# Expert weight pairs in six pairs of places instead of four, and the adding step cut into two halves around the next up products

## The chip, the cores and the metric

The kernel runs on one core of one Trainium2 chip. The time is the device time of one execution in microseconds (us); the runs of the kernel before took 2776.48 us in the median of three (2775.92 to 2777.67). Profiles come from one profiled execution.

## The reference

Two transformer blocks run one after the other over 256 tokens of width 1024, all in float32. The first has feed-forward layers, a gated delta rule and sparse attention. The second, over 272 rows (16 meta tokens ahead), is: fox attention, a mixture of experts, a gated recurrence (hg), a mixture of experts. Only the two mixtures matter here:

```python
def hier_moe(h, w_grp, b_grp, w_rt, b_rt, w_up, w_down):
    ...
    e_val, e_idx = lax.top_k(e_logit, TOP_K)          # 2 of 32 experts per token
    gate = jax.nn.softmax(e_val, axis=-1) * g_gate
    ...
    def expert_block(args):
        xb, e = args
        gate_up = xb @ w_up[e]                        # 1024 x 1024
        a, u = jnp.split(gate_up, 2, axis=-1)
        return (jax.nn.silu(a) * u) @ w_down[e]       # 512 x 1024
    ...
```

Each mixture reads the weights of all 32 experts, 6 MB each in float32.

## The kernel before

**Weights.** All weights come from HBM as slabs of 128 partitions x 2048 float32 (1 MB), in one fixed order, `plan`. SP alone issues their DMAs, in that order (L546 for two slabs at once, L550 for one). They land in `ring`, which has RING = 8 places; slab i goes to place i % 8, and `load(i)` first waits for the semaphore value at which slab i - 8 has been used. SP stands at that wait, and everything behind it in SP's queue stands too.

**The expert slabs** are loaded two by two, 2 MB a DMA. In this text a *pair* is such a DMA, numbered from 0 in each mixture. Pairs 0 and 1 are the up weights of expert 0 (rows 0 to 511, then 512 to 1023 of the 1024), pairs 2 and 3 those of expert 1. Then, for e = 1, 2, ...: two up pairs of expert e + 1 and one down pair of expert e. Pair 94, the last one, is the down pair of expert 31. The down weights of expert 0 are apart (`aside`, L559, two DMAs of 1 MB): before pair 4 SP waits until the sum of squares of the mixture's norm is there (`ss_ready`), and then loads them into the storage of `sq` and a part of `arena`. So the ring holds four pairs, and pair j waits for the products of pair j - 4.

**The order on TensorE** (sparse_pe) is written out by hand. For each expert e: `up_part(e + 1, 0)` (L1331, 16 products with an up pair), `turn(e)` (L1340, two transposes), `combine(e - 1)` (L1372, the adding step: four times, i = 0 to 3, a spread of expert e - 1's result over the tokens, into two banks of PSUM each), `up_part(e + 1, 1)` (L1331), for e < 3 a part of a gather (L1296), and `down_part(e)` (L1356, 16 products with the down pair). The first product of each of these waits for its own slab. Four of PSUM's banks serve the adding step, so its steps i = 2 and 3 wait until VectorE has added i = 0 and 1:

```python
                        if n >= 4:
                            pe.wait_ge(s["moe_x"], MOE_ADDS * l + 2 * (n - 2))
```

**On VectorE** (sparse_dve) each expert has `take_turn(e)` (L3026), `add(e - 1)` (L3047, four additions onto x), `gate_rows(e)` (L3033 twice, L3039) and `hidden_e(e + 1)` (L3019). **On ScalarE** (sparse_act): SiLU (L2100), the rows of expert e + 2 (L2093), and the result of the down products out of PSUM (L2106, `take_y`).

**Ahead of the experts** the mixture is normed, routed (L1402, the transposes of `h` at L1250, marked "htok") and sorted. In the waits of the sort, `keep_clock` (L1256) runs products that nobody reads, with `h` as operand. A second version of each mixture, dense_pe and its like, runs only when an expert has more than 64 rows. It did not run here: the lines of the profile are those of the sparse one.

`sq`, `hid` and `sil` are scratch of the norms, the feed-forward, the attention and hg; the sparse mixture touches none of them after its norm.

Of the kernel before, what the change touches and what calls it, by code (L numbers as in the profile page):

```python
# [8 lines left out]
P = 128  # L9
D = 1024  # L10
KC = D // P
# [171 lines left out]
def arrivals(plan):  # L183

    count, out = [0] * RING, []
    for i in range(len(plan)):
        slot = i % RING - (1 if i and paired(plan, i - 1) else 0)
        if slot == i % RING:
            count[slot] += 1
        out.append((slot, 16 * count[slot]))  # L190
    return out
# [254 lines left out]
def build(nc, ap, stages, marks):  # L446
    plan = slab_plan(stages)
    free, arrive = releases(plan), arrivals(plan)
    with ExitStack() as ctx:
# [12 lines left out]
        sq = sb("sq", [P, KC, T2])  # L462
        hid = sb("hid", [P, 2, 2, T2])
        sil = sb("sil", [P, 2, T2])
# [13 lines left out]
        def view(at, *shape, whole=arena):  # L478
            n = int(np.prod(shape))
            v = whole[:, at:at + n]  # L480
            if len(shape) == 1:
# [7 lines left out]
                 (sq.rearrange("p k n -> p (k n)")[:, 0:SLAB], view(21264, SLAB))]  # L489
# [12 lines left out]
        slot_loaded = [sem(f"slot{i}_loaded") for i in range(RING)]  # L502
# [5 lines left out]

        def slab_view(i, k=KC):
            return ring[:, i % RING, :].rearrange("p (k n) -> p k n", k=k)  # L510

        def low_view(i, k=KC):
            return ring_parts[:, i % RING, :].rearrange("p (k n) -> p k n", k=k)
# [12 lines left out]
        def _(sp):  # L526
# [11 lines left out]
            def load(i):  # L538
                if i >= RING:
                    name, value = free[i - RING]  # L540
                    sp.wait_ge(s[name], value)
                if paired(plan, i):
                    name, value = free[i + 1 - RING]
                    sp.wait_ge(s[name], value)
                    both = ap["slabs"][i:i + 2].rearrange("n p w -> (n p w)").rearrange("(p w) -> p w", p=P)
                    sp.dma_start(ring[:, i % RING:i % RING + 2, :].rearrange("p n w -> p (n w)"), both)\  # L546
                        .then_inc(slot_loaded[i % RING], 16)
                    return
                w = slab_width(plan[i])
                sp.dma_start(ring[:, i % RING, 0:w], ap["slabs"][i, :, 0:w]).then_inc(slot_loaded[i % RING], 16)  # L550

            edges = list(itertools.accumulate(len(slab_plan([st])) for st in stages))
            moe_at = {at - 6 * NE + 2 + RING: q for q, (at, st) in enumerate(zip(edges, stages)) if st[0] == "moe"}
            for i in range(len(plan)):
                if i in moe_at:
                    q = moe_at[i]
                    sp.wait_ge(s["ss_ready"], sum(r[0] != "ada" for r in stages[:q + 1]))
                    for hh in range(2):
                        sp.dma_start(aside[hh].rearrange("p k n -> p (k n)"), ap["aside"][2 * stages[q][1] + hh])\  # L559
                            .then_inc(s["aside_in"], 16)  # L560
                if not (i and paired(plan, i - 1)):
                    load(i)
# [125 lines left out]
        HTLO = 18144  # L688
        LG, SEL, GOH, GCAND, GEXP, EL, ECAND, EL2, TOP1, TOP2 = (RT, RT + 108, RT + 236, RT + 248, RT + 260, RT + 272,
# [47 lines left out]
        def sum_slab(eng, i):  # L737
# [3 lines left out]
            wt = ring[:, i % RING, :].rearrange("p (f k) -> p f k", f=2)  # L741
# [9 lines left out]
        def _(pe):  # L751
# [6 lines left out]
            def slab_in(i):  # L758

                slot, at = arrive[i]  # L760
                pe.wait_ge(slot_loaded[slot], at if trip[0] is None else trip[0] * (24 // RING * 16) + at)
# [3 lines left out]
            def run_jobs(q, st, lo, hi, slab, job, rhs=h, h_at=None, behind=False):  # L765
# [3 lines left out]
                for i, (kind, idx, sl, c0, _) in list(enumerate(stage_jobs(st)))[lo:hi]:  # L769
# [51 lines left out]
                    elif kind in ("vtok", "gba", "fv", "hv"):  # L821
# [3 lines left out]
                        if kind == "gba":  # L825
                            wt = ring[:, nth_slab(st, slab, sl) % RING, 0:KC * 32].rearrange("p (k n) -> p k n", k=KC)
# [485 lines left out]
            def sparse_pe(q, l, slab):  # L1312
# [66 lines left out]
                for e in range(NE):  # L1379
# [3 lines left out]
                    if e:  # L1383
                        combine(e - 1)
# [2022 lines left out]
```

## Time and profile before

| | |
|---|---|
| median of 3 runs | 2776.48 us |
| the profiled execution, its time | 2777.99 us |
| its span | 2776.2 us |
| what lies around the span | 1.8 us |
| mean granted TensorE clock | 0.98 |
| bytes read from HBM | 697.46 MB |
| DMAs of 2 MB, one of 1 MB | 190 and 278 |

The span is cut into 40 slices of 69.4 us in the page's second part. The first mixture lies in slices 23 to 29 (about 1534 to 2038 us), the second from slice 33 to the end (2264 to 2773 us). A busy share there is an average over the slice.

### The profile page before, as it was taken

How to read it: one execution, taken by the hardware profiler on the slowest of the kernel's cores; microseconds unless marked ns; L12 is line 12 of the kernel's file. 1: busy time of each engine (PE TensorE's matmuls, PEld its weight loads, DVE VectorE, ACT ScalarE, POOL GpSimd, SP SyncE). 2: the span in 40 equal slices, each digit the busy share in tenths (PEclk: the TensorE clock that was granted, in tenths of full speed). 3: DMA queues.
4: the chain of work that ended last, by engine and by line, in shares of the span. 5: the costliest groups of instructions: out<-in, count | busy, mean ns of one | idle time of the engine just before them, and what ended most of it. 6: DMA issues, size and time to landing. Idle time of an engine off the chain costs nothing.

```text
span 2776.2 us, 44780 instructions
## 1 busy us (share of the span) xinstructions
PE 2624.0 (95%) x18738; PEld 1897.1 (68%) x18738; DVE 1387.0 (50%) x2815; ACT 767.8 (28%) x1478; POOL 0.2 (0%) x4
## 2 busy tenths in 40 slices
PE   7999989999999989999999999999999999999998
PEld 7999868999999868998777533333367784333333
DVE  7875865776773764753233433333324542323333
ACT  4331444344331353433233211101112331111010
POOL 0000000000000000000000000000000000000000
PEclk9999989999999999999999999999999999999999
DMA  9877301774776311554211599999961238999997
GB/s 365 319 269 275 122 33 64 293 293 189 309 278 245 120 51 62 213 197 159 84 61 47 227 398 428 427 428 427 428 251 60 92 122 325 419 429 427 428 427 316
DMA packets 72353, 701.51 MB, mean 253 GB/s; under 512 B 8784, under 2 KB 11472, under 8 KB 11728
## 3 DMA queue, kind: packets, MB, share of 16 engines
q1 hardware_dynamic: 72144, 698.54, 62.8%
q8 instruction: 154, 2.52, 0.4%
q14 instruction: 55, 0.45, 0.0%
HBM read 697.46 MB, written 1.05 MB: 252 GB/s over the span
## 4 chain that ended last, share of the span: by engine, by line
PE 85%; DVE 6%; DMA 4%; ACT 3%; issue 2%; SPq 0%; DVEq 0%; ACTq 0%
PE ps L1331 15%; PE ps L837 12%; PE ps L1532 9%; PE ps L1530 9%; PE ps L1531 8%; PE ps L1356 7%; PE ps L1372 4%; DMA ring<-slabs 4%; PE ps L828 4%; PE ps L1084 2%; DVE x L3047 2%; PE ps L1509 1%; PE ps L819 1%; PE ps L804 1%; PE ps L1261 1%
## 5 line engine op out<-in xcount | busy, mean ns | idle before, releaser
L1530 PE MATMUL ps<-arena_parts 128*128 128x256 f32 x2032 | 575.8, 283 | 0.4 <-DVE arena_parts L3210 0.4
L1532 PE MATMUL ps<-arena_parts,ring_parts 128*128 128x256 f32 x2032 | 573.2, 282 | 0.0
L1531 PE MATMUL ps<-arena_parts 128*128 128x256 f32 x2032 | 571.5, 281 | 0.0
L1331 PE MATMUL ps<-ring,arena 128*64 128x512 f32 x2048 | 469.0, 599 | 42.7 <-ACT arena L2106 30.3
L1531 PEld LDWEIGHTS ps<-arena_parts 128*128 128x128 f32 x2032 | 385.9, 190 | 0.2
L1530 PEld LDWEIGHTS ps<-arena_parts 128*128 128x128 f32 x2032 | 383.4, 189 | 0.8 <-DVE arena_parts L3210 0.6
L1532 PEld LDWEIGHTS ps<-arena_parts,ring_parts 128*128 128x128 f32 x2032 | 382.7, 188 | 0.0
L1331 PEld LDWEIGHTS ps<-ring,arena 128*64 128x64 f32 x2048 | 147.8, 137 | 326.2 <-issue 260.6
L3199 DVE TENSOR_TENSOR ring_parts<-ring,arena_parts 128x2048 fp32r<-128x2048 f32 x132 | 300.8, 2290 | 109.1 <-ACT arena_parts L1723 108.9
L1723 ACT CAST arena_parts<-ring 128x2048 fp32r<-128x2048 f32 x132 | 250.4, 1905 | 302.1 <-DMA ring<-slabs 295.1
L837 PE MATMUL ps<-h,ring 128*128 128x256 f32 (+1 forms) x1408 | 328.4, 391 | 3.7 <-DVE h L3191 3.5
L837 PEld LDWEIGHTS ps<-h,ring 128*128 128x128 f32 x1408 | 266.4, 192 | 49.9 <-issue 5.3
L3026 DVE COPY arena<-ps 128x256 f32<-128x256 f32 x64 | 27.2, 424 | 459.3 <-PE ps L1340 459.3
L1356 PE MATMUL ps<-ring,arena 128*64 128x512 f32 x992 | 223.7, 593 | 0.0
L2100 ACT ACTIVATE arena<-ps 128x256 f32<-128x256 f32 x64 | 24.6, 384 | 662.9 <-PE ps L1331 662.9
L3047 DVE TENSOR_TENSOR x<-ps,x 128x544 f32<-128x544 f32 x256 | 173.5, 720 | 41.8 <-PE ps L1372 26.8
L1372 PE MATMUL ps<-arena 64*128 64x272 f32 x1024 | 163.0, 428 | 29.3 <-DVE x L3047 27.2
L744 DVE CUSTOM_DVE_ANT_0 ring<-ring,arena,vectors 128x1024 f32<-128x1024 f32 x144 | 176.9, 1279 | 10.1 <-DMA ring<-slabs 10.1
L1356 PEld LDWEIGHTS ps<-ring,arena 128*64 128x64 f32 x992 | 70.7, 137 | 139.5 <-issue 139.0
L1372 PEld LDWEIGHTS ps<-arena 64*128 64x128 f32 x1024 | 82.6, 185 | 94.6 <-DVE x L3047 75.7
L828 PE MATMUL ps<-ring,h 128*128 128x256 f32 (+3 forms) x576 | 115.2, 357 | 0.0
L828 PEld LDWEIGHTS ps<-ring,h 128*128 128x128 f32 (+1 forms) x576 | 84.6, 175 | 22.9 <-issue 2.6
(415 smaller groups left out, 2545.5 us busy)
## 6 DMA issues: line engine op xcount, KB each, us to landing
ring<-slabs SPq DMA_DIRECT2D x190, 2048.0 KB, 14.8
ring<-slabs SPq DMA_DIRECT2D x278, 1024.0 KB, 5.3
sq<-aside SPq DMA_DIRECT2D x2, 1024.0 KB, 8.6
arena<-aside SPq DMA_DIRECT2D x2, 1024.0 KB, 10.7
x<-xT SPq DMA_DIRECT2D x1, 1024.0 KB, 5.6
outT<-x SPq DMA_DIRECT2D x4, 256.0 KB, 2.7
constants<-const SPq DMA_DIRECT2D x1, 875.0 KB, 7.7
vectors<-vec SPq DMA_DIRECT2D x1, 647.5 KB, 7.2
```

Source lines behind the costliest of these rows:

```text
L744: ins = nc.vector.tensor_tensor_reduce(out=wt[:, f], in0=wt[:, f], in1=cond_row, scale=1.0, scalar=col("ada_b", l * NADA + n), op0=ALU.mul ...
L828: mm = nc.tensor.matmul(ps[0:size, b, 0:width], rhs[:, k, at:at + size], wt[:, k, c0:c0 + width], start=(k == 0), stop=(k == KC - 1))
L837: mm = nc.tensor.matmul(bank(b, n), wt[:, k, c0:c0 + P], rhs[:, k, 0:n], start=(k == ks[0]), stop=(k == ks[-1]))
L1331: mm = nc.tensor.matmul(ps[W * hh:W * hh + W, e % 2, :], rows_of, wt[:, c], start=(k == 0 and c == 0), stop=(k == 1 and c == 3))
L1356: mm = nc.tensor.matmul(ps[W * dh:W * dh + W, 3, :], hide[:, e % 2, j, W * hh:W * hh + W], wt[:, j, 512 * dh:512 * dh + 512], start=(hh == ...
L1372: mm = nc.tensor.matmul(ps[:, 4 + 2 * (i % 2) + dh, 0:T2], ysb[rows64, e % 2, i * P:(i + 1) * P], ge[rows64, e % 2], start=True, stop=True)
L1530: nc.tensor.matmul(out, w_hi, v_hi, start=start, stop=False, skip_group_check=True)
L1531: nc.tensor.matmul(out, w_hi, v_lo, start=False, stop=False, skip_group_check=True)
L1532: return nc.tensor.matmul(out, w_lo, v_hi, start=False, stop=stop, skip_group_check=True)
L1723: nc.scalar.copy(hi_slab(i), slab_view(i)).then_inc(s["w_hi"], 1)
L3047: nc.vector.tensor_tensor(two, ps[:, b:b + 2, 0:T2], two, ALU.add).then_inc(s["moe_x"], 4)
L3199: nc.vector.tensor_tensor(low_view(i), wt, hi_slab(i).bitcast(F32), ALU.subtract)\
```

## The change

- `places(plan)` gives each slab its place in place of i % 8. In a mixture the pairs go round over six pairs of places: pairs 0 to 3 of each six take the next eight places of the ring, pairs 4 and 5 take four new places (8, 9 and 10, 11) in a tensor `more`. All other slabs go round the ring as before. `load(i)` waits for the slab that had the place before, `before_it[i]`.
- `sq`, `hid` and `sil` become views of the upper half of `more` (places 10 and 11). The room comes from `dynamic_dma_scratch_size=1024`.
- SP's order: pair 4 is loaded ahead of pair 0. Where pair 4 stood nothing is done. Where pair 5 stood, SP waits for `ss_ready`, loads pair 5, then the first aside slab, waits until the last transposes of `h` are done, and loads the second aside slab, now over `h`.
- From e = 4 on, `combine(e - 1)` does i = 0 and 1 ahead of `up_part(e + 1, 1)` and i = 2 and 3 behind it. VectorE's `add` is cut the same way, around `gate_rows(e)`.
- `keep_clock` reads constants. The dense version gets its own copies of `h`, `hid` and `sil`.

```diff
+def places(plan):
+
+    out, at, n = [], 0, 0
+    for i, s in enumerate(plan):
+        n = (n + 1 if i and plan[i - 1][0] in ("eup", "edown") else 0) if s[0] in ("eup", "edown") else 0
+        if s[0] in ("eup", "edown") and n // 2 % 6 >= 4:
+            out.append(RING + 2 * (n // 2 % 6 - 4) + n % 2)
+        else:
+            out.append(at % RING)
+            at += 1
+    return out
...
+def earlier(place):
+
+    last, out = {}, []
+    for i, p in enumerate(place):
+        out.append(last.get(p))
+        last[p] = i
+    return out
+
+
+def arrivals(plan, place):
+
+    count, out = [0] * (RING + 4), []
+    for i, p in enumerate(place):
+        second = i and paired(plan, i - 1)
+        count[p - 1 if second else p] += 0 if second else 1
+        out.append((p - 1 if second else p, 16 * count[p - 1 if second else p]))
     return out
...
-    free, arrive = releases(plan), arrivals(plan)
+    place = places(plan)
+    free, arrive, before_it = releases(plan), arrivals(plan, place), earlier(place)
...
-        sq = sb("sq", [P, KC, T2])
-        hid = sb("hid", [P, 2, 2, T2])
-        sil = sb("sil", [P, 2, T2])
+        more = sb("more", [P, 4, SLAB])
+        wide = more[:, 2:4, :].rearrange("p n w -> p (n w)")
+        sq = wide[:, 0:KC * T2].rearrange("p (k n) -> p k n", k=KC)
+        hid = wide[:, KC * T2:(KC + 4) * T2].rearrange("p (a b n) -> p a b n", a=2, b=2)
+        sil = wide[:, (KC + 4) * T2:(KC + 6) * T2].rearrange("p (a n) -> p a n", a=2)
...
         aside = [v.rearrange("p (k n) -> p k n", k=2) for v in
-                 (sq.rearrange("p k n -> p (k n)")[:, 0:SLAB], view(21264, SLAB))]
+                 (view(21264, SLAB), h.rearrange("p k n -> p (k n)")[:, 0:SLAB])]
...
-        slot_loaded = [sem(f"slot{i}_loaded") for i in range(RING)]
+        slot_loaded = [sem(f"slot{i}_loaded") for i in range(RING + 4)]
...
+        def slab_place(i, n=1):
+
+            p = place[i]
+            return ring[:, p:p + n, :] if p < RING else more[:, p - RING:p - RING + n, :]
+
         def slab_view(i, k=KC):
-            return ring[:, i % RING, :].rearrange("p (k n) -> p k n", k=k)
+            return slab_place(i)[:, 0].rearrange("p (k n) -> p k n", k=k)
...
             def load(i):
-                if i >= RING:
-                    name, value = free[i - RING]
+                if before_it[i] is not None:
+                    name, value = free[before_it[i]]
                     sp.wait_ge(s[name], value)
                 if paired(plan, i):
-                    name, value = free[i + 1 - RING]
-                    sp.wait_ge(s[name], value)
+                    if before_it[i + 1] is not None:
+                        name, value = free[before_it[i + 1]]
+                        sp.wait_ge(s[name], value)
                     both = ap["slabs"][i:i + 2].rearrange("n p w -> (n p w)").rearrange("(p w) -> p w", p=P)
-                    sp.dma_start(ring[:, i % RING:i % RING + 2, :].rearrange("p n w -> p (n w)"), both)\
-                        .then_inc(slot_loaded[i % RING], 16)
+                    sp.dma_start(slab_place(i, 2).rearrange("p n w -> p (n w)"), both).then_inc(slot_loaded[place[i]], 16)
                     return
                 w = slab_width(plan[i])
-                sp.dma_start(ring[:, i % RING, 0:w], ap["slabs"][i, :, 0:w]).then_inc(slot_loaded[i % RING], 16)
+                sp.dma_start(ring[:, place[i], 0:w], ap["slabs"][i, :, 0:w]).then_inc(slot_loaded[place[i]], 16)
             edges = list(itertools.accumulate(len(slab_plan([st])) for st in stages))
-            moe_at = {at - 6 * NE + 2 + RING: q for q, (at, st) in enumerate(zip(edges, stages)) if st[0] == "moe"}
+            moe_at = {at - 6 * NE + 2: q for q, (at, st) in enumerate(zip(edges, stages)) if st[0] == "moe"}
             for i in range(len(plan)):
                 if i in moe_at:
-                    q = moe_at[i]
+                    load(i + 8)
+                if i - 8 in moe_at:
+                    continue
+                if i - 10 in moe_at:
+                    q = moe_at[i - 10]
                     sp.wait_ge(s["ss_ready"], sum(r[0] != "ada" for r in stages[:q + 1]))
+                    load(i)
                     for hh in range(2):
+                        if hh:
+                            sp.wait_ge(s["pe_step"], marks.value("pe_step", (q, "htok", 5)))
                         sp.dma_start(aside[hh].rearrange("p k n -> p (k n)"), ap["aside"][2 * stages[q][1] + hh])\
                             .then_inc(s["aside_in"], 16)
-                if not (i and paired(plan, i - 1)):
+                elif not (i and paired(plan, i - 1)):
                     load(i)
...
-            wt = ring[:, i % RING, :].rearrange("p (f k) -> p f k", f=2)
+            wt = ring[:, place[i], :].rearrange("p (f k) -> p f k", f=2)
...
-                    nc.tensor.matmul(bank(b, T2), ident, h[:, 0, 0:T2], start=True, stop=True)
+                    nc.tensor.matmul(bank(b, T2), ident, const[:, 0:T2], start=True, stop=True)
...
-                def combine(e):
-                    if e < 3:
-                        await2("act", q, "xs", 1, PIECES[e][-1])
-                    await2("act", "ysb", e)
-                    await2("dve", "ge", e)
-                    for i in range(4):
+                def combine(e, pairs):
+                    if pairs[0] == 0:
+                        if e < 3:
+                            await2("act", q, "xs", 1, PIECES[e][-1])
+                        await2("act", "ysb", e)
+                        await2("dve", "ge", e)
+                    for i in pairs:
                         n = 8 * e + 2 * i
                         if n >= 4:
                             pe.wait_ge(s["moe_x"], MOE_ADDS * l + 2 * (n - 2))
...
@@ -1381,9 +1419,11 @@
                         up_part(e + 1, 0)
                     turn(e)
                     if e:
-                        combine(e - 1)
+                        combine(e - 1, (0, 1) if e > 3 else range(4))
                     if e + 1 < NE:
                         up_part(e + 1, 1)
+                    if e > 3:
+                        combine(e - 1, (2, 3))
                     if e < 3:
                         if e == 0:
                             await2("dve", "rows")
@@ -1392,7 +1432,7 @@
                         gather(q, 1, mark2, lambda engine, *key: (await2 if engine == "act" else await_)(engine, *key),
                                (4, 5, 6, 7), PIECES[e])
                     down_part(e)
-                combine(NE - 1)
+                combine(NE - 1, range(4))
...
-                                    mm = nc.tensor.matmul(bank(b + f, T2), wt[:, c, at:at + P], h[:, 4 * kk + c, 0:T2],
+                                    mm = nc.tensor.matmul(bank(b + f, T2), wt[:, c, at:at + P], dense_h[:, 4 * kk + c],
...
+                await2("dve", "h")
...
-                def add(e):
-                    for i in range(4):
+                def add(e, pairs):
+                    for i in pairs:
                         await2("pe", "add", e, i)
                         if e:
                             dve.wait_ge(s["moe_x"], MOE_ADDS * l + 2 * (8 * (e - 1) + 2 * i + 2))
...
@@ -3053,11 +3094,13 @@
                 for e in range(NE):
                     take_turn(e)
                     if e:
-                        add(e - 1)
+                        add(e - 1, (0, 1) if e > 3 else range(4))
                     gate_rows(e)
+                    if e > 3:
+                        add(e - 1, (2, 3))
                     if e + 1 < NE:
                         hidden_e(e + 1)
-                add(NE - 1)
+                add(NE - 1, range(4))
...
+                for c in range(KC):
+                    ins = nc.vector.scalar_tensor_tensor(out=dense_h[:, c], in0=x[:, c], scalar=col("moe_g", KC * l + c),
+                                                         in1=rstd[:, 0:T2], op0=ALU.mult, op1=ALU.mult)
+                mark2(ins, "h")
...
-        nc = bacc.Bacc("TRN2", target_bir_lowering=False, num_devices=1)
+        nc = bacc.Bacc("TRN2", target_bir_lowering=False, num_devices=1, dynamic_dma_scratch_size=1024)
```

## Rows read from the trace of the kernel before

**Rows 1.** The page's second part: busy tenths, clock, DMA and GB/s in 40 slices.
```profile
PE   7999989999999989999999999999999999999998
...
PEclk9999989999999999999999999999999999999999
DMA  9877301774776311554211599999961238999997
GB/s 365 319 269 275 122 33 64 293 293 189 309 278 245 120 51 62 213 197 159 84 61 47 227 398 428 427 428 427 428 251 60 92 122 325 419 429 427 428 427 316
```

**Rows 2.** Windows of both mixtures: busy us, then PEclk, DMA share, GB/s.
```profile
1533.00:1565.00 32.00, 28.35 (x156) 20.44 (x156) 19.28 (x67) 9.08 (x21) 0.00 (x0) 0.95 0.33 129
1565.00:1613.00 48.00, 47.14 (x249) 21.37 (x246) 13.47 (x25) 5.88 (x14) 0.00 (x0) 1.00 0.90 349
1613.00:1640.00 27.00, 26.15 (x135) 9.96 (x135) 9.21 (x17) 3.48 (x7) 0.00 (x0) 1.00 0.98 381
1640.00:2034.00 394.00, 363.83 (x1775) 133.29 (x1772) 130.25 (x244) 43.07 (x82) 0.00 (x0) 1.00 1.01 427
2297.00:2345.00 48.00, 47.14 (x249) 21.20 (x246) 13.48 (x25) 5.88 (x14) 0.00 (x0) 1.00 0.90 349
```

**Rows 3.** DMA issues of L546: pairs 4 to 94 of the first mixture.
```profile
L546 SPq DMA_DIRECT2D ring<-slabs x91: 327/328/328, 1565.0 to 2011.5; - x91
...
DMA to landing us min/median/max: 7.6/14.9/17.1
```

**Rows 4.** The chain of the first mixture: starts of products of an up pair.
```profile
1624.10 3.58 PE ps L1331 x16
1637.82 3.58 PE ps L1331 x16
1651.54 3.58 PE ps L1331 x16
...
1672.90 3.65 PE ps L1331 x16
...
1687.58 3.65 PE ps L1331 x16
...
1702.26 3.65 PE ps L1331 x16
```

**Rows 5.** The issue of pair 91 (and its time to landing).
```profile
L546 SPq DMA_DIRECT2D ring<-slabs x1: 328/328/328, 1996.8 to 1996.8; - x1
...
DMA to landing us min/median/max: 15.1/15.1/15.1
```

**Rows 6.** TensorE at the end of the first mixture, from pair 91's products.
```profile
2012.12 3.65 PE L1331 MATMUL ps<-ring,arena 128*64 128x512 f32 x16 [0.73 <-ACT arena L2106]
2015.71 0.44 PE L1340 MATMUL ps<-constants,arena 128*128 128x128 f32 x2
2016.08 1.19 PE L1372 MATMUL ps<-arena 64*128 64x272 f32 x8
2017.69 1.36 PE L1372 MATMUL ps<-arena 64*128 64x272 f32 x8 [0.42 <-DVE x L3047]
2018.98 3.65 PE L1331 MATMUL ps<-ring,arena 128*64 128x512 f32 x16
2022.46 3.60 PE L1356 MATMUL ps<-ring,arena 128*64 128x512 f32 x16
2025.99 0.44 PE L1340 MATMUL ps<-constants,arena 128*128 128x128 f32 x2
2026.75 1.19 PE L1372 MATMUL ps<-arena 64*128 64x272 f32 x8 [0.32 <-ACT arena L2106]
2028.36 1.36 PE L1372 MATMUL ps<-arena 64*128 64x272 f32 x8 [0.42 <-DVE x L3047]
2029.65 3.65 PE L1356 MATMUL ps<-ring,arena 128*64 128x512 f32 x16
```

**Rows 7.** TensorE in the second mixture: an early expert, and the last up products.
```profile
2355.99 3.65 PE L1331 MATMUL ps<-ring,arena 128*64 128x512 f32 x16
...
2752.86 3.65 PE L1331 MATMUL ps<-ring,arena 128*64 128x512 f32 x16
```

**Rows 8.** SP's queue ahead of the first mixture, in order of time.
```profile
1410.17 0.33 SPq L550 DMA_DIRECT2D ring<-slabs  x1
1444.32 87.90 SPq L546 DMA_DIRECT2D ring<-slabs  x4
1533.68 0.33 SPq L559 DMA_DIRECT2D sq<-aside  x1
1534.06 0.48 SPq L559 DMA_DIRECT2D arena<-aside  x1
1565.05 0.33 SPq L546 DMA_DIRECT2D ring<-slabs  x1
```

**Rows 9.** The first mixture's start in order of time: transposes of h, first products.
```profile
1539.93 2.40 PE L1250 MATMUL ps<-constants,h 128*128 128x128 f32 x20
...
1561.32 7.09 PE L1331 MATMUL ps<-ring,arena 128*64 128x512 f32 x32 [1.53 <-ACT arena L2082]
```

**Rows 10.** DVE in one expert of the steady stretch, in order of time.
```profile
2001.51 0.42 DVE L3026 COPY arena<-ps 128x256 f32<-128x256 f32 x1 [7.35 <-PE ps L1340]
2002.23 1.36 DVE L3047 TENSOR_TENSOR x<-ps,x 128x544 f32<-128x544 f32 x2 [0.30 <-PE ps L1372]
2003.84 1.36 DVE L3047 TENSOR_TENSOR x<-ps,x 128x544 f32<-128x544 f32 x2 [0.25 <-PE ps L1372]
2005.12 0.91 DVE L3033 SCALAR_TENSOR_TENSOR arena<-arena,constants 128x272 f32<-128x272 f32 x2
2006.13 0.44 DVE L3039 TENSOR_TENSOR arena<-arena 128x272 f32<-128x272 f32 x1
2008.43 0.42 DVE L3019 TENSOR_TENSOR arena<-ps,arena 128x256 f32<-128x256 f32 x1 [1.85 <-ACT arena L2100]
```

**Rows 11.** Around the only fall of the clock within a mixture's stream.
```profile
1840.00:1855.00 15.00, 12.75 (x54) 4.50 (x56) 3.58 (x7) 1.60 (x3) 0.00 (x0) 0.89 1.01 429
...
1850.60 5.35 PE L1331 MATMUL ps<-ring,arena 128*64 128x512 f32 x16 [2.25 <-DMA ring<-slabs]
```

**Rows 12.** hg: its first products, and the issues of its later slabs (L550).
```profile
2043.58 12.61 PE L837 MATMUL ps<-h,ring 128*128 128x272 f32 x54 [1.74 <-DVE h L3191]
...
L550 SPq DMA_DIRECT2D ring<-slabs x8: 327/328/328, 2051.2 to 2102.5; - x8
```

More of the change, by code:

```diff
@@ L180, in paired @@
     return plan[i][0] in ("eup", "edown") and plan[i + 1:i + 2] and plan[i + 1][0] in ("eup", "edown") and i % 2 == 0
[L183 to L190, printed above, removed]
+def places(plan):
[20 more added lines that the diff above has]
+        out.append((p - 1 if second else p, 16 * count[p - 1 if second else p]))
     return out
@@ L688, in build @@
         HTLO = 18144
+        dense_h, dense_hid, dense_sil = view(SILE, KC, T2), view(SILE + KC * T2, 2, 2, T2), view(XE, 2, T2)
         LG, SEL, GOH, GCAND, GEXP, EL, ECAND, EL2, TOP1, TOP2 = (RT, RT + 108, RT + 236, RT + 248, RT + 260, RT + 272,
@@ L760, in slab_in @@
                 slot, at = arrive[i]
-                pe.wait_ge(slot_loaded[slot], at if trip[0] is None else trip[0] * (24 // RING * 16) + at)
+                pe.wait_ge(slot_loaded[slot], at if trip[0] is None else trip[0] * 32 + at)
             mark, await_ = stepper("pe")
@@ L825, in run_jobs @@
                         if kind == "gba":
-                            wt = ring[:, nth_slab(st, slab, sl) % RING, 0:KC * 32].rearrange("p (k n) -> p k n", k=KC)
+                            wt = ring[:, place[nth_slab(st, slab, sl)], 0:KC * 32].rearrange("p (k n) -> p k n", k=KC)
                         for k in range(KC):
@@ L1451, in down @@
                         for f in range(2):
-                            mm = nc.tensor.matmul(bank(4 + i % 2, T2), wt[:, f, d * P:(d + 1) * P], hid[:, hh, f, 0:T2],
+                            mm = nc.tensor.matmul(bank(4 + i % 2, T2), wt[:, f, d * P:(d + 1) * P], dense_hid[:, hh, f],
                                                   start=(f == 0), stop=(f == 1))
@@ L2158, in step @@
                             w(f"d_up{l}", u // 4 * 3 + u % 4 + 1, 12)
-                        nc.scalar.activation(sil[:, f, 0:T2], bank(f, T2), ACT.Silu).then_inc(s[f"d_silu{l}"], 1)
+                        nc.scalar.activation(dense_sil[:, f], bank(f, T2), ACT.Silu).then_inc(s[f"d_silu{l}"], 1)
                 await2("pe", "gt")
@@ L3128, in gated @@
                         w(f"d_silu{l}", u + 1, 16)
-                        nc.vector.tensor_tensor(hid[:, par, f, 0:T2], bank(2 + f, T2), sil[:, f, 0:T2], ALU.mult)\
+                        nc.vector.tensor_tensor(dense_hid[:, par, f], bank(2 + f, T2), dense_sil[:, f], ALU.mult)\
                             .then_inc(s[f"gated{l}"], 1)
                         w(f"gated{l}", 2 * k + f + 1, 16)
-                        nc.vector.tensor_tensor(hid[:, par, f, 0:T2], hid[:, par, f, 0:T2],
+                        nc.vector.tensor_tensor(dense_hid[:, par, f], dense_hid[:, par, f],
                                                 view(GBC, 2, T2)[:, k // 2 % 2], ALU.mult)\
```

2 lines of the change are left out of this document (1 added, 1 removed).

## The prediction

> **What bounds the kernel now.** I read the 40 slices first: in both mixtures the DMA row stands at 9 and the rate at 427 to 428 GB/s for slice after slice, while TensorE is at 9 too, so the slices alone do not say which of the two ends last [rows 1]. Windows split the mixture by stage: while 1565 to 1613 us has a DMA share of 0.90, the long stretch from 1640 to 2034 us has 1.01 at 427 GB/s, and TensorE is busy 364 of its 394 us [rows 2]. The chain of waits gives the pace: the products of an up pair start 13.7 us apart at first (1624.10, 1637.82, 1651.54) and 14.7 us apart from about 1673 us on (1672.90, 1687.58, 1702.26) [rows 4]. An expert takes three pairs of 2.097 MB. At 427 GB/s a pair takes 4.91 us and three take 14.7 us. So 13.72 us is TensorE's own pace and 14.7 us is the stream's: from the seventh expert or so the weight stream sets the end, and TensorE waits about 0.7 us an expert ahead of an up product [rows 6]. (That wait stands there as one on ScalarE, but the work it names ended long before; pair 91 was issued at 1996.8 us and took 15.1 us to land, 2011.9 us, and its products start at 2012.12 us [rows 5, 6].)
>
> What is the stream's length? It starts when the first products free places (the issue at 1565.05 us) and carries pairs 4 to 94, 91 of them, the last issued at 2011.5 us [rows 3, 8]. Ahead of it the DMA engines are nearly free: 0.33 of the time from 1533 to 1565 us, and 33 to 64 GB/s in some slices of the stages before [rows 1, 2]. Bytes moved from the stream into that idle time shorten the mixture.
>
> **The change, part by part.**
>
> *Six pairs of places.* Pair 4 goes into new places that nobody held, so SP issues it right behind the single slab of 1410.17 us, ahead of pair 0 at 1444.32 us. Pair 5 goes out with the aside slabs at 1533.7 us [rows 8]. The stream then starts with pair 6, and pair 6 waits for what pair 4 waited for: the products of pair 0. In general pair m + 6 is released by the same products as pair m + 4 before. 89 pairs are left instead of 91: 2 x 4.91 = 9.8 us less for each mixture, **19.6 us** in both. Bounds: the share of 0.90 and 0.98 in the first 75 us [rows 2] is a loss of 48 x 0.10 + 27 x 0.02 = 5.3 us for want of freed places. Since the releases are the same products, I leave it as it is; at best it goes wholly, at worst each mixture gains only the pair that is not loaded at the last moment, 4.9 us.
>
> *Are the extra pairs there in time?* Behind `ss_ready` stand pair 5 and two aside slabs, 4.19 MB or 9.8 us at 427 GB/s, over by about 1548 us with a latency like the 7.6 us of a lone pair [rows 3]. The first products start at 1561.32 us and the first to need pair 5 are those of expert 2 [rows 9]. Nil.
>
> *The new wait ahead of the second aside slab.* The transposes of `h` end at 1539.93 + 2.40 = 1542.3 us [rows 9]. Behind this wait on SP stand the aside slab, needed by the first down products (behind the up products that start at 1561.32 us), and pair 6, which cannot go before 1565.05 us anyway. Nil; without that cover it would be 1542.3 - 1534.06 = 8.3 us.
>
> *Pair 4 ahead of pair 0 in SP's queue* puts 4.91 us of transfer ahead of one wanted more than 100 us later [rows 8, 9]. Nil.
>
> *The adding step in halves.* Before, the four steps take 2016.08 to 2018.98 us, 2.90 us, with a wait of 0.42 us on VectorE's additions; the first two steps alone take 1.19 us [rows 6]. Two halves without the wait are 2.4 us, so TensorE's own pace falls from 13.72 to about 13.2 us. The stream is the bound at 14.7 us, so within the mixture this is hidden: it only widens the pause. It pays at the end. Before, the down products of expert 31 start 17.8 us after pair 91 has landed (2011.9 to 2029.65 us) [rows 5, 6]. After: 0.2 + 3.6 + 0.4 for the products and the turn, 1.2 for a half, 3.5 for pair 92 (landed at 4.9), 1.2 for a half; then pair 93 (landed at 9.8) at 10.1, 3.5 of down products, 0.8 to the last cut step, 2.9 for it (at e = 31 nothing lies between its halves): 17.3 us. **0.5 us** for each mixture, 1.0 in both. Bounds: nothing, and 1.0 us each (the waits of weight loads on the additions could go too).
>
> *VectorE behind it.* `hidden_e(e + 1)` now queues behind the second half. Before it ends 0.9 us behind the up products (2007.96 to 2008.85 us); after, it follows products of 1.2 us and a last addition of 0.7 us and ends some 2.5 us behind them [rows 6, 10]. Its reader, the next turn, lies behind 3.5 us of down and 3.6 us of up products. Covered, with over 4 us to spare; with the cover gone it would be 1.6 us an expert.
>
> *Other stages.* hg's first eight slabs follow pair 94 in the stream: 8 x 2.46 = 20 us after about 2017 us, and hg's products start at 2043.58 - 10.3 = 2033.3 us and take a slab in 7.3 us [rows 12]. Six have landed by then. Nil. The dense copies do not run; `keep_clock`, the views and the smaller scratch change operands only. Nil, within the 1 to 2 us by which executions differ.
>
> **TensorE must not become the bound.** Without any gain from the halves the up products of expert 31's second pair could start 27 paces after 1624.10 us: 1624.10 + 27 x 13.72 = 1994.5 us. The stream allows them at 2018.98 - 9.8 = 2009.2 us. In the second mixture it is 2355.99 + 370.4 = 2726.4 against 2743.1 us [rows 6, 7]. TensorE has 15 us to spare in each, so the stream stays the bound and the pairs' 9.8 us come through even without the halves.
>
> **The sum.** 19.6 + 1.0 = 20.6 us off the profiled execution's 2777.99 us gives 2757.4 us. The median of the runs lies 1.5 us under it: 2755.9, **2756 us**, own range 2753 to 2759.
>
> The row for the stream's rate is 427 GB/s. The Trainium skill ("DMA: Bandwidth & Descriptors", Specifications) puts the HBM limit of one core at about 358 GB/s. By that a pair would take 5.9 us and the two mixtures would gain 23.4 us, an estimate from that page; the trace disagrees, and the sum goes by the trace.
>
> **Rivals.**
>
> *TensorE is the bound after all.* That happens from a pace of (2009.2 - 1624.1) / 27 = 14.26 us on. At 14.4 it costs 27 x 0.14 = 3.8 us for each mixture: 2763.5 us. For it: TensorE is busy 92% already. Against it: 13.72 us in the rows. 0.06.
>
> *The early loss shrinks.* Two more pairs in flight could keep the DMA engines fuller through the first experts, up to 5.3 us more for each mixture: 2745 us. Against it: the releases are unchanged. 0.06.
>
> *The change does not do what it says:* pairs 4 and 5 are not in the idle time, or the transfers make up the time elsewhere: no change, 2776 us. 0.04.
>
> *Slower: the clock.* TensorE will idle more, near 1.4 us in one piece ahead of an up product. The only low clock within a stream, 1.2 GHz for a part of 1840 to 1855 us, came behind a pause of 2.25 us, and the group of products took 5.35 instead of 3.65 us, 1.7 us more [rows 6, 11]. One such fall in an expert gives 13.2 + 1.7 = 14.9 us, about the stream's pace. Two give 16.6, 1.9 us too many, and 6 experts of that eat a mixture's 10.3 us. For 25 experts in each mixture it is 95 us: 2851 us. Against it: one fall in more than 50 experts, with pauses of 0.7 us in nearly all. 0.03. The Trainium skill ("TensorE: Matmul & The Clock Gate", Part 1) says that the throttled state is the default and that activity releases it, which is the direction of this rival; no stretch here shows the pace under longer pauses.
>
> **The numbers.** Forecast 0.81, the rivals 0.06, 0.06, 0.04, 0.03. The range of 2750 to 2764 us holds the forecast, its unknown bounds and the first rival. A change of under 0.2%, 5.5 us, is about what a measurement here cannot tell from none. Faster: 0.81 + 0.06 + 0.06 = 0.93; within: 0.04; slower: 0.03.
>
> **What would show it.** In the profile after, 89 issues from the first mixture's first release (about 1565 us) to its last, a median time to landing near 25 us (five pairs in flight); the pace of up products still 14.7 us late in the mixture, reached later than before; hg's first products near 2033 us; the wait of the adding step on VectorE gone for experts 3 to 29. The prediction is wrong if the pace lies above 14.7 us, if the clock falls again and again between 1640 and 2034 us, or if pair 5 or an aside slab shows up in a wait of TensorE near 1580 us.

## The result: 0.99 of the time before; the mixtures give about what was worked out, and some 5 us more come from ahead of them

| | before | after |
|---|---|---|
| median us (4 runs each) | 2777.07 (2775.92 to 2780.58) | 2752.23 (2751.24 to 2753.22) |
| ratio, 95% interval | | 0.9901 (0.9882 to 0.9919) |
| span of the profiled execution | 2776.2 | 2750.3 |
| first issue of the stream, first mixture | 1565.05 | 1559.70 |
| first issue of the stream, second mixture | 2297.03 | 2282.71 |

The forecast was 2756 us. The last two rows cut the 25.9 us between the spans into three parts. Up to the first mixture's stream: 5.35 us. From there to the second stream: 731.98 against 723.01 us, 8.97 us. From there to the end: 479.2 against 467.6 us, 11.6 us. The last two together are 20.6 us, the sum that was forecast. (Each holds a mixture and what follows it: hg in the one, the end of the kernel in the other.) The 5.35 us lie ahead of every line that the change was meant to make faster.

Windows of the kernel after, in the columns of [rows 2]. The first three are moved by the 5.35 us, so that they lie about the start of the stream as those of [rows 2] do:

```profile
1527.70:1559.70 32.00, 28.55 (x157) 20.50 (x157) 19.28 (x67) 9.08 (x21) 0.00 (x0) 0.95 0.50 198
1559.70:1607.70 48.00, 47.14 (x250) 21.42 (x247) 13.46 (x25) 5.87 (x14) 0.00 (x0) 1.00 0.91 350
1607.70:1634.70 27.00, 26.57 (x134) 10.01 (x135) 7.87 (x15) 3.86 (x8) 0.00 (x0) 1.00 0.97 383
1640.00:2020.00 380.00, 353.79 (x1752) 131.06 (x1750) 127.27 (x242) 42.18 (x79) 0.00 (x0) 1.00 1.01 427
```

More is moved ahead of the stream: 198 GB/s where it was 129, which over 32 us is 2.2 MB, one pair. The first 75 us fall short of a full stream just as before (350 and 383 GB/s, where they were 349 and 381), and then the rate is the same 427 GB/s. The issues of the first mixture's stream (L576 is the new line of L546):

```profile
L576 SPq DMA_DIRECT2D ring<-slabs x60: 327/328/328, 1559.7 to 1982.0; - x60
L576 SPq DMA_DIRECT2D more<-slabs x29: 327/328/328, 1583.3 to 1987.0; - x29
...
DMA to landing us min/median/max: 7.6/25.2/26.9
```

60 + 29 = 89 pairs where there were 91, and a median of 25.2 us from issue to landing where it was 14.9: five pairs are now in flight late in the mixture, three were before [rows 3]. The chain of the first mixture (the work that ended last, followed back) says when the stream becomes the bound:

```profile
1630.66 3.58 PE ps L1368 x16
1643.86 3.58 PE ps L1368 x16
1657.07 3.58 PE ps L1368 x16
...
1735.80 25.39 DMA ring<-slabs
1761.53 3.67 PE ps L1368 x16
1765.26 25.30 DMA ring<-slabs
1790.81 3.67 PE ps L1368 x16
```

L1368 is L1331 of before. Its products come 13.2 us apart, TensorE's own pace with the cut step, until about 1735 us. Only then does the chain go through the DMAs, 29.3 us for two experts, which is the old 14.7 us each. In [rows 4] the change came near 1670 us. The end of the first mixture, against [rows 6]:

```profile
1997.88 3.65 PE L1368 MATMUL ps<-ring,arena 128*64 128x512 f32 x16 [1.23 <-DMA ring<-slabs]
2001.47 0.44 PE L1377 MATMUL ps<-constants,arena 128*128 128x128 f32 x2
2001.84 1.19 PE L1410 MATMUL ps<-arena 64*128 64x272 f32 x8
2002.95 3.65 PE L1368 MATMUL ps<-ring,arena 128*64 128x512 f32 x16
2006.54 1.19 PE L1410 MATMUL ps<-arena 64*128 64x272 f32 x8
2007.65 3.65 PE L1393 MATMUL ps<-ring,arena 128*64 128x512 f32 x16
2011.24 0.44 PE L1377 MATMUL ps<-constants,arena 128*128 128x128 f32 x2
2011.99 1.19 PE L1410 MATMUL ps<-arena 64*128 64x272 f32 x8 [0.32 <-ACT arena L2147]
2013.61 1.36 PE L1410 MATMUL ps<-arena 64*128 64x272 f32 x8 [0.43 <-DVE x L3088]
2014.90 3.65 PE L1393 MATMUL ps<-more,arena 128*64 128x512 f32 x16
```

Up to the step of expert 29 the adding step stands in two pieces of 1.19 us around the up products, with no wait on VectorE. From 1640 to 1990 us the weight loads of this step waited 28.4 us for VectorE's additions in the kernel before; in the changed kernel no such wait is left. From the products of pair 91 to the down products of expert 31 it is 17.0 us (1997.88 to 2014.90); before, it was 17.5 us (2012.12 to 2029.65).

The 5.35 us ahead of all this come from the feed-forward stages of the first block. The same window of both kernels (before first), with TensorE busy throughout and at the same clock:

```profile
600.00:830.00 230.00, 229.03 (x1898) 227.91 (x1897) 173.19 (x220) 91.86 (x84) 0.00 (x0) 1.00 0.67 260
```
```profile
600.00:830.00 230.00, 228.94 (x1918) 227.83 (x1917) 172.05 (x219) 91.99 (x83) 0.00 (x0) 1.00 0.69 263
```

There are 1918 products where there were 1898, 1.05% more, and no instruction of that stage differs but in the places of its operands in SBUF.

### The profile page after: what moved, and what is told of

It reads as the page before. It is cut to its first block, busy times and chain, and to the rows that moved or that the text cites. A ratio compares the mean times of both kernels' runs of the same rounds, so it can differ in the third digit from the quotient of the medians.

```text
span 2750.3 us, 44778 instructions
## 1 busy us (share of the span) xinstructions
PE 2612.2 (95%) x18738; PEld 1890.9 (69%) x18738; DVE 1381.7 (50%) x2815; ACT 767.5 (28%) x1478; POOL 0.2 (0%) x4
## 3 DMA queue, kind: packets, MB, share of 16 engines
HBM read 697.46 MB, written 1.05 MB: 254 GB/s over the span
## 4 chain that ended last, share of the span: by engine, by line
PE 74%; DMA 17%; DVE 5%; ACT 2%; issue 2%; SPq 0%; DVEq 0%; ACTq 0%
PE ps L874 12%; PE ps L1368 10%; DMA ring<-slabs 9%; PE ps L1572 9%; PE ps L1573 9%; PE ps L1571 9%; DMA more<-slabs 8%; PE ps L865 4%; PE ps L1393 3%; PE ps L1410 2%; PE ps L1121 2%; PE ps L1550 1%; PE ps L856 1%; PE ps L841 1%; PE ps L1298 1%
## 5 line engine op out<-in xcount | busy, mean ns | idle before, releaser
L1368 PE MATMUL ps<-ring,arena 128*64 128x512 f32 x1088 | 248.0, 597 | 25.3 <-DMA ring<-slabs 20.2
L1368 PE MATMUL ps<-more,arena 128*64 128x512 f32 x960 | 221.9, 604 | 24.5 <-DMA more<-slabs 24.5
L1393 PE MATMUL ps<-ring,arena 128*64 128x512 f32 x960 | 219.1, 598 | 1.4 <-DVE arena L3060 1.4
L1368 PEld LDWEIGHTS ps<-ring,arena 128*64 128x64 f32 x1088 | 78.1, 136 | 173.0 <-issue 131.9
L1368 PEld LDWEIGHTS ps<-more,arena 128*64 128x64 f32 x960 | 69.1, 138 | 159.6 <-issue 124.5
L1410 PE MATMUL ps<-arena 64*128 64x272 f32 x1024 | 153.7, 417 | 6.3 <-DVE x L3088 4.3
L1393 PEld LDWEIGHTS ps<-ring,arena 128*64 128x64 f32 x960 | 64.2, 136 | 124.9 <-issue 124.4
## 6 DMA issues: line engine op xcount, KB each, us to landing
ring<-slabs SPq DMA_DIRECT2D x128, 2048.0 KB, 25.2
```

Of the source, the lines that this page charges most:

```text
L1368: mm = nc.tensor.matmul(ps[W * hh:W * hh + W, e % 2, :], rows_of, wt[:, c], start=(k == 0 and c == 0), stop=(k == 1 and c == 3))
L1393: mm = nc.tensor.matmul(ps[W * dh:W * dh + W, 3, :], hide[:, e % 2, j, W * hh:W * hh + W], wt[:, j, 512 * dh:512 * dh + 512], start=(hh == ...
L1410: mm = nc.tensor.matmul(ps[:, 4 + 2 * (i % 2) + dh, 0:T2], ysb[rows64, e % 2, i * P:(i + 1) * P], ge[rows64, e % 2], start=True, stop=True)
```

## The experiments

Eight kernels were timed in three rounds (the number of runs is given), two were run once. On the chip of the first four the kernel before took 2777.76 us in the median of 25 runs (2770.45 to 2786.53), on that of the others 2779.70 us in 7 (2774.12 to 2784.23), so differences of 2 us between medians say nothing. The trace separates the parts better. For each profile, *ff* is the length of the three stretches of feed-forward products together, from the first start to the last start in each (before: 192.2 + 387.1 + 190.4 us). *T0* is the first issue of the first mixture's stream, *M1* the time from there to that of the second, and *M2* from there to the end of the span. *products* is TensorE's count in the window from 600 to 830 us, and *clock* the granted clock in that from 1285 to 1555 us. A run's own medians and ratios stand with it.

| | ff | T0 | M1 | M2 | products | clock |
|---|---|---|---|---|---|---|
| before | 769.6 | 1565.1 | 732.0 | 479.2 | 1898 | 0.96 |
| after | 762.5 | 1559.7 | 723.0 | 467.6 | 1918 | 0.95 |
| e1 places only | 761.9 | 1565.1 | 723.8 | 468.2 | 1918 | 0.93 |
| e2 halves only | 770.1 | 1564.1 | 732.5 | 477.3 | 1898 | 0.96 |
| e3 scratch only | 769.9 | 1565.7 | 733.9 | 478.2 | 1899 | 0.95 |
| e4 arena moved, from before | 761.9 | 1563.1 | 733.3 | 477.6 | 1917 | 0.94 |
| e5 late pairs | 762.5 | 1558.7 | 722.5 | 467.7 | 1917 | 0.95 |
| e6 five pairs | 762.0 | 1557.9 | 726.6 | 472.7 | 1917 | 0.95 |
| e7 arena 128 bytes on | 769.9 | 1564.0 | 724.7 | 468.0 | 1898 | 0.96 |
| e8 arena 64 bytes on | 761.7 | 1559.2 | 724.6 | 467.5 | 1917 | 0.95 |
| e9 moving operands 128 bytes on | 773.8 | 1567.5 | 725.1 | 467.0 | 1886 | 0.95 |
| e10 weights 128, moving operands 256 bytes on | 775.4 | 1570.3 | 723.2 | 467.6 | 1886 | 0.95 |

The *ff* of the kernel before, e2, e3 and e7 is 769.6 to 770.1 us, that of the changed kernel, e1, e4, e5, e6 and e8 is 761.7 to 762.5 us, some 8 us less, and between the kernel before and the changed one it is 7.1 us. T0 holds the other stages too. Outside *ff* they take 793.7 to 797.5 us, but 803.2 us in e1 and 801.1 us in e4, the two profiles with the lowest clock in the attention (0.93 and 0.94). The late T0 of e1, 1565.1 us, goes with that clock. *M1* and *M2* scatter too: over the three profiles that have neither the places nor the halves (before, e3, e4), *M1* differs by 1.9 us and *M2* by 1.6.

SP's queue in the last feed-forward stage, in the order before, after, e1, shows the same. It is 6.2 to 6.3 us ahead at the first of these issues and 6.8 to 6.9 us at the end of the last:

```profile
1233.35 64.90 SPq L550 DMA_DIRECT2D ring<-slabs  x13
```
```profile
1227.09 64.26 SPq L579 DMA_DIRECT2D ring<-slabs  x13
```
```profile
1227.15 64.26 SPq L579 DMA_DIRECT2D ring<-slabs  x13
```

### e1: the places without the halves

```diff
-                        combine(e - 1, (0, 1) if e > 3 else range(4))
+                        combine(e - 1, range(4))
...
-                    if e > 3:
-                        combine(e - 1, (2, 3))
```

and the same for VectorE's `add`.

> The changed kernel with the adding step whole again (six pairs of places, new SP order and new layout stay). Theory 'the stream is the bound': the places give 9.8 us for each mixture by themselves and the halves only shorten the last expert, so about 1 us over the changed kernel: 2753 us, the pace of up products early in the mixture 13.7 us and 14.7 us later. Rival 'TensorE would be the bound without the halves': the pace stays above 14.26 us from the first experts on and the time is 2757 us or more.

Measured: 2750.94 us (4 runs, 2745.07 to 2758.84), ratio 0.9899 (0.9875 to 0.9923), no different from the changed kernel. M1 and M2 are 0.7 and 0.6 us longer, which is within their scatter. TensorE's early pace is the old one:

```profile
1624.10 3.65 PE L1368 MATMUL ps<-more,arena 128*64 128x512 f32 x16
...
1637.83 3.65 PE L1368 MATMUL ps<-ring,arena 128*64 128x512 f32 x16
...
1651.55 3.65 PE L1368 MATMUL ps<-more,arena 128*64 128x512 f32 x16
```

13.7 us apart, and still M1 and M2 are 8.2 and 11.0 us shorter than before. TensorE was not the bound without the halves. The rival falls. At the end of the first mixture, from the products of pair 91 to the down products of expert 31:

```profile
2002.74 3.65 PE L1368 MATMUL ps<-ring,arena 128*64 128x512 f32 x16 [0.73 <-ACT arena L2145]
...
2020.28 3.65 PE L1393 MATMUL ps<-more,arena 128*64 128x512 f32 x16
```

That is 17.5 us, as in the kernel before. With the halves it is 17.0 us, in the changed kernel and in e2 alike (2010.53 to 2027.54 us there).

### e2: the halves without the places

The edit is the change's part in `sparse_pe` and `sparse_dve`, put into the kernel before.

> The kernel before with the adding step in halves and nothing else. Theory 'the stream is the bound': TensorE's early pace falls from 13.7 to 13.2 us, the late one stays at 14.7 us, and only the last expert gains: 2775.5 us. Rival 'the halves carry a part of the gain': 2771 us or less.

Measured: 2779.45 us (10 runs), ratio 1.0004 (0.9990 to 1.0018). M1 is 0.5 us longer and M2 1.9 us shorter than before, no more than their scatter. The early pace fell as expected:

```profile
1635.04 3.65 PE L1331 MATMUL ps<-ring,arena 128*64 128x512 f32 x16
1638.62 1.19 PE L1373 MATMUL ps<-arena 64*128 64x272 f32 x8
1639.74 3.65 PE L1356 MATMUL ps<-ring,arena 128*64 128x512 f32 x16
...
1648.24 3.65 PE L1331 MATMUL ps<-ring,arena 128*64 128x512 f32 x16
```

13.2 us instead of 13.7, and nothing in the time that stands out of the noise. The halves free TensorE's time where TensorE has time to spare.

### e3: the scratch alone

```diff
-        nc = bacc.Bacc("TRN2", target_bir_lowering=False, num_devices=1)
+        nc = bacc.Bacc("TRN2", target_bir_lowering=False, num_devices=1, dynamic_dma_scratch_size=1024)
```

> The kernel before with the smaller scratch and nothing else. The changed kernel reached its first mixture 5.3 us earlier than the kernel before, and in the feed-forward stages its products follow each other after 118 ns in place of 119 to 120. Theory 'smaller scratch, or the shift it gives to all tensors': the first mixture is reached 5 us earlier, 2771 us. Rival 'the place of arena against the other tensors': no change, 2776.5 us. Rival 'chance of the run': the first mixture's start scatters by some us over all these kernels.

Measured: 2777.66 us (10 runs), ratio 1.0005 (0.9991 to 1.0020); T0 is 1565.7 us. The size of the scratch, and whatever shift it gives to all tensors together, does nothing that can be measured. The count of products is the old one within one. Chance does not explain the 5.35 us either: over all twelve profiles the count follows the layout to within one product.

### e4: arena moved by 128 bytes

```diff
+        sb("gap", [P, 32])
         arena, arena_parts = twice("arena", [P, 21640 + 4 * COLS + 2 * T1 + DEPTH * NADA])
```

on top of e3. The new layout puts 8192 floats a partition (`more`) where `sq`, `hid` and `sil` had 3808, so arena moved by 17536 bytes, which is 68 x 256 + 128.

> As the run before, with an unused tensor of 128 bytes a partition ahead of arena, so that arena alone is moved by an odd multiple of 128 bytes, as in the changed kernel. Theory 'the place of arena sets the pace of the feed-forward products': 118 ns from product to product and the first mixture reached 5 us earlier, 2771 us. Rivals 'scratch' and 'chance': the same as the run with the scratch alone.

Measured: 2771.71 us (10 runs), ratio 0.9969 (0.9955 to 0.9982), clearly faster than e3 on the same chip, by 6 us. The window of the feed-forward stage:

```profile
600.00:830.00 230.00, 228.94 (x1917) 227.83 (x1916) 171.16 (x218) 92.00 (x83) 0.00 (x0) 1.00 0.68 262
```

1917 products: the changed kernel's pace, from 128 unused bytes, and an *ff* 8.0 us shorter than that of e3. M1 and M2 are within 1.6 us of the kernel before. (T0 in this profile is only 2 us earlier. SP's first aside slab went out at 1529.61 against 1533.68 us, 4 us earlier; the rest was lost behind it, where the clock in the window from 1555 to 1562 us is 0.76.)

### e5: the two extra pairs not loaded ahead of time

```diff
-                if i in moe_at:
-                    load(i + 8)
                 if i - 8 in moe_at:
                     continue
...
                     sp.wait_ge(s["ss_ready"], sum(r[0] != "ada" for r in stages[:q + 1]))
-                    load(i)
...
                             .then_inc(s["aside_in"], 16)
+                    name, value = free[i - 10]
+                    sp.wait_ge(s[name], value)
+                    load(i - 2)
+                    load(i)
```

> The changed kernel, with pairs 4 and 5 not loaded ahead of time: SP issues both only when the products of pair 0 are done, directly ahead of pair 6. Six pairs of places stay. Theory 'bytes moved into the idle time ahead of the stream' (the prediction's words): the stream is two pairs longer again, 9.8 us for each mixture, 2772 us. Rival 'the two more pairs in flight cover TensorE's slow first experts': the stream then starts with two pairs more but no longer runs dry in the first 75 us, where it lost some 9 us, and the last pair lands as early as in the changed kernel: 2752 us, within 3 us.

Measured: 2752.19 us (4 runs, 2746.84 to 2755.48), ratio 0.9900 (0.9876 to 0.9924): the changed kernel's time, to the microsecond. M1 and M2 are the same as well. Windows from the start of its stream, and the 95 us from there in the kernel before, the changed one and e5:

```profile
1558.70:1606.70 48.00, 47.14 (x249) 21.36 (x246) 13.47 (x25) 5.88 (x14) 0.00 (x0) 1.00 0.99 414
1606.70:1633.70 27.00, 26.58 (x135) 10.01 (x135) 7.87 (x15) 3.82 (x8) 0.00 (x0) 1.00 1.01 427
```
```profile
1565.10:1660.10 95.00, 92.86 (x476) 38.28 (x474) 27.95 (x52) 12.54 (x27) 0.00 (x0) 1.00 0.95 376
```
```profile
1559.70:1654.70 95.00, 93.71 (x482) 38.68 (x480) 27.75 (x52) 12.53 (x27) 0.00 (x0) 1.00 0.95 376
```
```profile
1558.70:1653.70 95.00, 93.71 (x482) 38.63 (x480) 27.76 (x52) 12.54 (x27) 0.00 (x0) 1.00 1.00 420
```

In these 95 us e5 moves 420 GB/s and the changed kernel 376. The difference is 4.2 MB, just the two pairs that the stream of e5 has more. So both streams stand at the same point 95 us after their start: one loses next to nothing for want of free places and carries 91 pairs, the other loses 11.3 us of 95 against 427 GB/s and carries 89. The words of my first theory, that the gain is bytes moved into idle time, fall with this run.

### e6: five pairs of places

```diff
-        if s[0] in ("eup", "edown") and n // 2 % 6 >= 4:
-            out.append(RING + 2 * (n // 2 % 6 - 4) + n % 2)
+        if s[0] in ("eup", "edown") and n // 2 % 5 >= 4:
+            out.append(RING + n % 2)
```

with pair 5 behind the aside slabs, so that it waits for the products of pair 0.

> The changed kernel with five pairs of places (places 10 and 11 are scratch only, pair 5 waits for the products of pair 0). Theory 'each pair of places is worth one pair of transfer': 4.9 us for each mixture back, 2762 us. Rival 'the fifth pair is enough to keep the stream full': 2752 us.

Measured: 2761.20 us (4 runs), ratio 0.9939 (0.9917 to 0.9962); M1 is 3.6 and M2 5.1 us over the changed kernel, 8.7 us together where two transfers of a pair are 9.8 us. Against the kernel before they are 5.4 and 6.5 us shorter. Each pair of places is worth about one pair of transfer.

### e7 and e8: arena 128 and 64 bytes further on in the changed kernel

```diff
+        sb("gap", [P, 32])    # e7; [P, 16] in e8
```

> The changed kernel with arena moved on by 128 bytes, back to the position modulo 256 that it had before. Theory 'the place of arena sets the pace of the feed-forward products': they follow each other after 121.3 ns in the mean in place of 120.1, and the time rises by 5 to 7 us to 2758 us. Rival 'another part of the new layout does it': 2752 us.

> The changed kernel with arena moved on by 64 bytes. Theory 'only the position modulo 128 or 256 matters': at 64 bytes off the mean distance of the feed-forward products is a third value or one of 120.1 and 121.3 ns; the time follows at about 5 us per ns. Rival 'another part of the layout': 120.1 ns and 2752 us.

Measured: 2759.98 us (4 runs), ratio 0.9928 (0.9904 to 0.9952) for e7; 2751.60 us (4 runs), ratio 0.9896 (0.9874 to 0.9918) for e8. The window in e7:

```profile
600.00:830.00 230.00, 229.04 (x1898) 227.93 (x1897) 171.57 (x220) 91.45 (x82) 0.00 (x0) 1.00 0.67 259
```

1898 products, the very count of the kernel before, and an *ff* 7.4 us longer than in the changed kernel. The median is 8 us over those of e5 and e8 on the same chip, but with four runs each the intervals of the ratios still overlap; it is the trace that shows the effect here, and e4 against e3 that shows it in the times. 64 bytes do not matter: e8 has 1917 products and an *ff* of 761.7 us.

### e9 and e10: which operand

```diff
-        HH_HI = HI_W + HI_RING * SLAB
+        HH_HI = HI_W + HI_RING * SLAB + 32
```

is e9; e10 has that and `HI_W = 5 * T1 + 32`, so that the weights move by 128 bytes and the moving operands by 256.

> The changed kernel, in which only the moving operands of the feed-forward products (the split h and hidden values at the end of that part of arena) lie 128 bytes further on; arena and the split weights stay. Theory 'the moving operand's position modulo 256 sets the pace': the mean distance of these products is 121.3 ns and the first mixture's stream starts 5 to 6 us later. Rival 'the weights' position': 120.1 ns.

> The changed kernel, in which the split weights lie 128 bytes and the moving operands 256 bytes further on. Theory 'the moving operand's position modulo 256 sets the pace': 120.1 ns, as in the changed kernel. Rival 'the weights' position': 121.3 ns. If both this run and the last are slower, it is the position of the one against the other.

Measured: one execution each, 2761.31 and 2762.96 us. Window of e9:

```profile
600.00:830.00 230.00, 229.12 (x1886) 227.99 (x1885) 170.83 (x218) 91.13 (x81) 0.00 (x0) 1.00 0.68 260
```

and of e10:

```profile
600.00:830.00 230.00, 229.11 (x1886) 227.99 (x1885) 170.60 (x217) 92.48 (x84) 0.00 (x0) 1.00 0.68 261
```

Both have 1886 products, fewer than the kernel before, and an *ff* of 773.8 and 775.4 us. Neither operand's position sets the pace alone: moved apart by 128 bytes in either way they are slower than in any kernel in which they kept their distance. That was the third case of the expectation. Why positions matter at all stays open. (The 120.1 and 121.3 ns of the expectations are near 230 us over 1918 and 1898 products, 119.9 and 121.2 ns, which hold the short pauses too. From start to start of products that follow at once, the trace has 117.8 ns in the changed kernel, 119.1 in the kernel before and 119.9 in e9 and e10.)

## Why the prediction was right and where it was wrong

**Right: the bound and its size.** The stream at 427 GB/s bound both mixtures behind their first experts (from about 1735 us on in the first), TensorE had time to spare, and M1 and M2 gave 20.6 us against 20.6 forecast (8.97 and 11.6 where each was put at 10.3). That the sum agrees to the tenth is luck, since M1 and M2 scatter by up to 2 us. e1 shows the places alone, 8.2 and 11.0 us. The halves are too small for the times. In the rows they are the forecast 0.5 us from the products of pair 91 to the last down products: 17.5 us without them (before, e1), 17.0 us with them (the changed kernel, e2). The signs asked for are there: 89 issues, a landing time near 25 us, a late pace of 14.7 us, no wait of the adding step on VectorE in the middle. hg's first products came at 2028.8 us for a forecast of 2033. That is 469.1 us behind T0, where it was 478.5 before: 9.4 us less for the first mixture, forecast 10.3; T0 itself came 5.35 us earlier.

**Wrong: "Other stages ... the views and the smaller scratch change operands only. Nil, within the 1 to 2 us by which executions differ."** This is the step that failed: a term put at nothing with no row for it. The three stretches of feed-forward products took 762.5 us where they took 769.6, 7.1 us less. The other stages ahead of the first mixture took 1.8 us more, which leaves 5.35 us at T0. The rearranged tensors moved arena by an odd multiple of 128 bytes, and the feed-forward products, which read both operands from arena or one from the ring, came 1% closer together. e4 gives the effect to the kernel before (*ff* 8.0 us shorter and 6 us on the median, against e3), and e7 takes it from the changed one (*ff* 7.4 us longer, 8 us on the median).

So the ratio is 0.9901 (a gain of 22 to 33 us by its interval), where 20.6 us would have been 0.9926, just outside. The median of 2752.2 us lies under my own range of 2753 to 2759 us, and 0.9901 of the 2776.48 us known at the time is 2749 us, under the 2750 of the wide range. That low end was set by what the mixtures could do and had no room for a gain in another stage.

**Right in size, wrong in its reason: "Bytes moved from the stream into that idle time shorten the mixture."** e5 loads nothing ahead and is as fast. What both kernels share is six pairs of places. Two things hold back the last pair. All pairs of the stream have to pass, at 4.91 us each. And when TensorE frees a place late in the slow first experts, all pairs still to come have to pass behind that release. Before, the second limit held: the stream had run short of places and moved 376 GB/s in its first 95 us. Two pairs of places more put two pairs less behind each release, and that is 9.8 us whether the stream starts with two pairs less (the changed kernel, again 376 GB/s) or never runs short (e5, 420 GB/s). I had written that pair m + 6 is released by the same products as pair m + 4 before, which was the right sum. e6 confirms it by one pair.

The rival "the early loss shrinks" did not happen in the changed kernel, whose rates from its T0 on are those of before; in e5, where it did, it was paid for by the two pairs more. The size of that loss was misread too. I took 5.3 us from the DMA share (0.90 and 0.98). The rates in the same rows, 349 and 381 against 427 GB/s, make it 11.7 us in those 75 us, and e5 shows that nearly all of it can go.

**The other rivals.** TensorE as the bound: e1 rules it out. The clock: TensorE does idle longer ahead of an up product, 1.2 us late in the mixture, and in this profile the clock fell twice in the second mixture, where it had not fallen before:

```profile
2587.39 5.20 PE L1368 MATMUL ps<-more,arena 128*64 128x512 f32 x16 [2.28 <-DMA more<-slabs]
```
```profile
2705.75 5.35 PE L1368 MATMUL ps<-more,arena 128*64 128x512 f32 x16 [2.23 <-DMA more<-slabs]
```

Both falls to 1.2 GHz came behind a pause of 2.2 to 2.3 us, as the one of [rows 11] did, and the products took 1.6 and 1.7 us longer. The Trainium skill ("TensorE: Matmul & The Clock Gate", Part 1) says that activity releases the throttle, and these rows agree in the direction: the clock fell behind pauses. It cost nothing that can be seen: M2 is 467.6 us here and 467.5 us in e8, where the clock of the second mixture did not fall.

## What to carry to other kernels

Where a transfer stream bounds a stage and TensorE is slow in its first steps, count the transfers still to come behind each release of a buffer. Each further buffer takes one off that count, and here it did not matter whether it was filled ahead of time. Time freed on the engine that is not the bound buys only the tail. And do not put a change of layout at nothing without a measurement: move a big tensor by 64 and 128 unused bytes by itself, before and after, and look at the number of products in a fixed window. When windows of two kernels are compared, lay them about the same event: the same window in clock time made the first 48 us of the stream look fuller here (356 GB/s from 1565 us on, 350 from T0 on).

## What was not expected of the hardware

In these runs the distance between back-to-back feed-forward products (128 x 256, type fp32r in the kernel) went with the place of their operands in SBUF. In 230 us of full TensorE at the same clock there were 1898 products in the kernel before and in e7, 1918 in the kernel after and 1917 in e4, 1886 in e9 and e10. Moving all of arena by 64 bytes changed nothing in T0 (1559.2 against 1559.7 us), moving it by 128 bytes changed the count by 18 to 20, and moving it back restored the old count exactly. Two things have a part: the distance of the two operands from each other (e9, e10), and the place of arena as a whole (e4, e7). Whether the second is its place against the ring or its own address is not separated. Nor is it known whether the products are slower by themselves or through ScalarE and VectorE, which write the split values into arena and the ring at the same time; no run here moved one without the other. Finer positions were not tried.
